# First units of two projections run on rows that the token's norm factor has not touched yet, one core of Trainium2

## The reference, cut to what matters

```python
def rmsnorm(x, w):
    inv = lax.rsqrt(jnp.mean(xf * xf, axis=-1, keepdims=True) + NORM_EPS)
    return (xf * inv) * w

h = rmsnorm(x, norm_mix_w)
a_b, a_c, a_x, z, xbc, dt_raw, g_a, g_b = split_in_proj(h @ w_in)
xbc_c = silu(causal_dwconv(xbc_full, ssd_conv_w) + ssd_conv_b)     # 4 taps
dt = softplus(dt_raw + ssd_dt_bias)                                # 32 heads
...
x = x + merged @ w_o
t = rmsnorm(x, norm_ffn_w)
q = (t @ w_q).reshape(..., PEER_HEADS, 2, PEER_HALF)               # then top 16 of 128 keys, experts
...
y = rmsnorm(x, norm_final_w)
```

## Time and profile before

| what | value |
|---|---|
| median of 3 runs | 2559.65 us (2555.63 to 2560.34) |
| the profiled execution's own time | 2555.39 us |
| its span, first to last instruction | 2553.4 us |
| mean granted TensorE clock | 0.979 |
| PE busy | 2461.1 us (96%) |
| DVE busy | 1640.5 us (64%) |
| ACT busy | 782.9 us (31%) |
| POOL busy | 1437.7 us (56%) |

### The profile page before, as it was taken

How to read it: one execution, slowest core, us unless ns; L and a number is a source line. 1 busy time by engine, 2 the same in 40 slices (tenths; PEclk the granted TensorE clock), 3 DMA queues, 4 the chain that set the end, 5 groups by cost and what they waited for, 6 DMA issues and landing times.

```text
span 2553.4 us, 38043 instructions
## 1 busy us (share of the span) xinstructions
PE 2461.1 (96%) x14490; PEld 2258.2 (88%) x14490; DVE 1640.5 (64%) x2612; ACT 782.9 (31%) x1188; POOL 1437.7 (56%) x787
## 2 busy tenths in 40 slices
PE   7899999999989998999999999999999999999997
PEld 6899899996678997999999999999988999999986
DVE  5787344545487423127988969889587666666663
ACT  2222112321112101123333345565533333332331
POOL 3455333432143454446766767777766777777762
PEclk8899999999999998999999999999999999999998
DMA  3223222224464232225766758988987888888861
GB/s 130 75 83 128 98 92 87 91 91 157 160 222 137 72 113 74 83 91 186 260 243 232 263 200 275 297 299 294 297 323 286 329 312 309 310 324 312 312 242 62
DMA packets 206252, 507.49 MB, mean 199 GB/s; under 512 B 15008, under 2 KB 103456, under 8 KB 203680
## 3 DMA queue, kind: packets, MB, share of 16 engines
q1 hardware_dynamic: 56496, 204.76, 25.0%
q10 hardware_dynamic: 112752, 166.56, 18.3%
q0 software_dynamic: 36864, 134.23, 14.2%
HBM read 422.06 MB, written 83.44 MB: 198 GB/s over the span
## 4 chain that ended last, share of the span: by engine, by line
PE 89%; DVE 6%; issue 2%; DMA 1%; ACT 1%; ACTq 0%; POOL 0%; DVEq 0%; POOLq 0%
PE ps L797 47%; PE ps L565 29%; PE ps L845 4%; PE ps L704 1%; PE ps L734 1%; PE ps L712 1%; PE ps L591 1%; DVE abuf L1732 1%; PE ps L810 1%; PE ps L716 1%; PE ps L719 1%; PE ps L692 0%; DMA gate_scratch<-gt 0%; DVE sp L1344 0%; DMA gbuf<-gate_scratch 0%
## 5 line engine op out<-in xcount | busy, mean ns | idle before, releaser
L514 POOL TENSOR_SCALAR w_hi<-raw 128x1024 fp32r<-128x1024 f32 x129 | 141.3, 1095 | 639.9 <-issue 508.5
L541 POOL TENSOR_TENSOR w_lo<-raw,w_hi 128x1024 fp32r<-128x1024 f32 x128 | 325.8, 2545 | 196.5 <-PE ps L797 196.3
L541 POOL TENSOR_TENSOR w_lo<-raw,e_hi 128x1024 fp32r<-128x1024 f32 x128 | 326.4, 2550 | 186.6 <-PE ps L797 179.7
L797 PE MATMUL ps<-p_hi,w_lo 128*128 128x448 f32 x1024 | 377.1, 368 | 0.0
L797 PE MATMUL ps<-g_hi,w_lo 128*128 128x448 f32 x1024 | 376.5, 368 | 0.0
L516 POOL TENSOR_TENSOR w_lo<-raw,w_hi 128x1024 fp32r<-128x1024 f32 x129 | 320.4, 2483 | 10.8
L565 PE MATMUL ps<-h_hi,w_hi 128*128 128x296 f32 (+1 forms) x1296 | 297.5, 311 | 18.6 <-ACT stage L941 9.6
L565 PE MATMUL ps<-h_lo,w_hi 128*128 128x296 f32 (+1 forms) x1296 | 283.1, 300 | 0.0
L565 PE MATMUL ps<-h_hi,w_lo 128*128 128x296 f32 (+1 forms) x1296 | 282.2, 299 | 0.0
L565 PEld LDWEIGHTS ps<-h_hi,w_hi 128*128 128x128 f32 x1296 | 212.5, 192 | 42.1 <-issue 24.5
L1118 ACT ACTIVATE e_hi<-raw 128x1024 fp32r<-128x1024 f32 x128 | 135.8, 1061 | 299.3 <-PE ps L797 117.1
(11 more groups left out here) (286 smaller groups left out, 5312.9 us busy)
## 6 DMA issues: line engine op xcount, KB each, us to landing
raw<-units SPq DMA_DIRECT2D x385, 512.0 KB, 3.7
gate_scratch<-gt ACTq DMA_DIRECT2D x14, 2048.0 KB, 12.7
gbuf<-gate_scratch ACTq DMA_DIRECT2D x32, 896.0 KB, 8.4
activation_scratch<-ge ACTq DMA_DIRECT2D x120, 224.0 KB, 3.1
abuf<-activation_scratch ACTq DMA_DIRECT2D x30, 896.0 KB, 5.9
prev<-ssm_in ACTq DMA_DIRECT2D x8, 1024.0 KB, 5.7
ssm_s<-prev ACTq DMA_DIRECT2D x8, 1024.0 KB, 4.4
parked_tiles<-stage ACTq DMA_DIRECT2D x24, 296.0 KB, 2.1
```

The lines of the kernel that those rows point to most:

```text
L514: pool.tensor_scalar(w_hi[:, s, :], raw[:, r, :], 1.0, 1.0, ALU.mult, ALU.mult).then_inc(s_whi, 1)
L541: pool.tensor_tensor(w_lo[:, n % 2, :], raw[:, n % RAW, :], e_hi[m % HS_].bitcast(F32), ALU.subtract)\
L797: last = mm(accp[par], w[:, k * P:(k + 1) * P], x_[:, k, t0:t0 + ND], start=k == 0 and i == 0, stop=k == KT - 1 and i == 2)
```

## The change

It touches the first norm, the norm ahead of the queries, and, through shared helpers, the last norm.

1. **Start.** The input loads are put in another order, with unit 0 ahead of x. x also comes token-major (`x_rows`, five tiles of 128 tokens by 1024). ACT makes `hu_hi` = x * w (rounded) and DVE `hu_lo`; no factor is in them. PE issues 20 matmuls of 128 x 128 on ones, then runs units 0 to 4 on `hu`. ACT squares the token-major rows with an accumulator output, which gives each token's sum at once on its own partition. `spread_out(0)` stands in the middle of unit 2. The factor is multiplied into dt (four pieces, L1447) and into the four parked tiles (`scale_stage`) by DVE. `normed` runs beside units 2 to 4, and units from 5 on use h as before.
2. **Softplus** is computed on 128 x 148 tiles (four token quarters on four groups of 32 partitions).
3. **ACT's order** is stage 0, hi parts 0 and 1, bias, abs and exp of dt, then hi parts, stages and stores in turn, and only then the wait for `s_sp`. The first convolution tap moves from DVE to ACT (L1030).
4. **Queries.** `gu_hi` (ACT) and `gu_lo` (DVE) are made while w_o still runs. Units 0 to 3 of w_q run on them; ACT copies them to `qu`, and DVE multiplies them by the factor after `normed`.
5. **Sums** ahead of the queries and at the end: `added_squares` contracts the 128 channels and turns in one step of eight small matmuls; the sum over ones, the row and `turn` are gone there.

```diff
@@ sync
+            sp_.dma_start(col[:], cols).then_inc(s_col, 16)
+            sp_.dma_start(raw[:, 0, :], units[0]).then_inc(ld[0], 16)
             for i in range(4):
                 sp_.dma_start(x[:, 2 * i:2 * i + 2], xT[:, 2 * i:2 * i + 2]).then_inc(s_x[i], 16)
+            sp_.dma_start(raw[:, 1, :], units[1]).then_inc(ld[1], 16)
+            for i in range(XR):
+                sp_.dma_start(rows[i][:], x_rows[:, i]).then_inc(s_xt[i], 16)
...
@@ tensor
             def added_squares(r):
                 pe.wait_ge(s_sqa, KT * (r - GROUPS))
-                for h in range(2):
-                    last = mm(ssp[:, h, 0:HK], ones, sqa[:, h * HK:(h + 1) * HK], start=True, stop=True)
-                last.then_inc(s_ss, 1)
+                nq = TK // NT
+                for i in range(NT):
+                    last = mm(turned[0:nq, i:i + 1], sqa[:, i * nq:(i + 1) * nq], ones[:, 0:1], start=True, stop=True)
+                last.then_inc(s_turn, 1)
...
-            square_sums(0)
-            turn(0)
+            for i in range(WARM):
+                mm(ps[:, 7, 0:P], ones_r[:], ones_r[:], start=True, stop=True)
+            hu = (hu_hi, hu_lo)
+            as_ready(U_DT, U_DT, hu, s_u, 0)
+            tile(U_DT + 1, U_DT + 1, *hu)
+            part(U_DT + 2, 0, 4, hu)
             spread_out(0)
-            two_tiles(U_DT, U_DT, (h_hi, h_lo), 0)
+            part(U_DT + 2, 4, KT, hu)
+            for n in range(U_DT + 3, N_RAW):
+                tile(n, n, *hu)
+            as_ready(N_RAW, N_RAW, (h_hi, h_lo), s_h, 0)
...
@@ scalar
+            def unscaled_hi(w, k, out):
+                act.activation(out[:, k, :], x[:, k, T - out.shape[2]:], ACT.Copy, scale=c_(w, k)).then_inc(s_uhi, 1)
...
+            for i in range(XR):
+                act.wait_ge(s_xt[i], 16)
+                act.activation(rows[i][:], rows[i][:], ACT.Square, accum_out=ss0[:, i:i + 1]).then_inc(s_us, 1)
...
@@ vector
+            def unscaled_lo(i0, w, k, hi, lo):
+                dve.wait_ge(s_uhi, i0 + k + 1)
+                stt(lo[:, k, :], x[:, k, T - lo.shape[2]:], c_(w, k), hi[:, k, :].bitcast(F32), ALU.mult, ALU.subtract)\
+                    .then_inc(s_u, 1)
...
+            def scale_stage(b):
+                n = PARKED[b]
+                dve.wait_ge(s_accf[n % 2], n // 2 + 1)
+                a = halves(stage[b % 2][:])
+                tt_(a, a, inv[:], ALU.mult).then_inc(s_scl, 1)
...
-            link(ts_(sp[1][:], sp[2][:], 2.0, None, ALU.add))
+            link(ts_(pk[1][:], pk[2][:], 2.0, None, ALU.add))
...
@@ vector, w_o and queries
+                if j >= 1:
+                    unscaled_lo(KT, "ffn", j - 1, gu_hi, gu_lo)
+            unscaled_lo(KT, "ffn", KT - 1, gu_hi, gu_lo)
             add_squares(1 + GROUPS, KT - 1)
...
             normed(1, "ffn", g_lo, g_hi)
+            for j in range(Q_RAW):
+                dve.wait_ge(s_qu, j + 1)
+                link(tt_(halves(q[:, j, :]), halves(qu[:, j, :]), inv[:, :, 0:HK], ALU.mult))
```

More of the change, by code:

```diff
@@ L217, in trunk @@
         dq = scr("dq", [P, T])
-        sp = [at(f"sp{i}", R_C + i * TW, [HEADS, T]) for i in range(4)]
         reset = scr("reset", [HEADS, T])
@@ L776, in _ @@
                 tile(U_WO + j, L_WO + j, m_hi, m_lo)
-            added_squares(1 + GROUPS)
-            turn(1 + GROUPS)
-            spread_out(1 + GROUPS)
-            two_tiles(U_WQ, U_WQ - L_SHIFT, (g_hi, g_lo), KT)
-            for j in range(2, N_WQ):
-                tile(U_WQ + j, U_WQ - L_SHIFT + j, g_hi, g_lo)
+            gu, L = (gu_hi, gu_lo), U_WQ - L_SHIFT
+            for k in range(KT):
+                if k == 6:
+                    added_squares(1 + GROUPS)
+                pe.wait_ge(s_u, KT + k + 1)
+                part(U_WQ, k, k + 1, gu, L)
+            part(U_WQ + 1, 0, 4, gu, L + 1)
+            spread_out(1 + GROUPS)
+            part(U_WQ + 1, 4, KT, gu, L + 1)
+            for j in range(2, Q_RAW):
+                tile(U_WQ + j, L + j, *gu)
+            as_ready(U_WQ + Q_RAW, L + Q_RAW, (g_hi, g_lo), s_h, KT)
+            for j in range(Q_RAW + 1, N_WQ):
+                tile(U_WQ + j, L + j, g_hi, g_lo)
             pe.wait_ge(s_q, N_WQ)
@@ new lines, in _ @@
+            dve.wait_ge(s_c, 1)
+            for k in range(KT):
+                unscaled_lo(0, "mix", k, hu_hi, hu_lo)
+            v, i, w = (root0[:, k, :] for k in range(3))
+            dve.wait_ge(s_us, XR)
+            ts_(v, ss0[:], 1.0 / D, EPS, ALU.mult, ALU.add).then_inc(s_vt, 1)
+            inverse_root(0, v, i, w)
+            n = T // P
+            diagonals(P, n, i[:, 0:n])
+            tt_(spread[:, n * P:T], ident[:, 0:T - n * P], i[:, n:n + 1].to_broadcast([P, T - n * P]), ALU.mult)\
+                .then_inc(s_diag, 1)
@@ new lines, in _, with scale_parked @@
+            dve.memset(reset[:], 1.0)
+            dve.wait_ge(s_inv, 1)
+            dve.wait_ge(s_accf[0], 1)
+            wq = T // 4
+            for i in range(4):
+                last = tt_(pk[0][HEADS * i:HEADS * (i + 1), :], sp[0][:, i * wq:(i + 1) * wq],
+                           inv[0:HEADS, i // 2, i % 2 * wq:(i % 2 + 1) * wq], ALU.mult)
+            last.then_inc(s_dts, 1)
+            def scale_parked(k):
+                b = {0: 0, 4: 1, 7: 2}.get(k)
+                if b is None:
+                    return
+                scale_stage(b)
```

274 lines of the change are left out of this document (168 added, 106 removed).

## The result

| | before | changed |
|---|---|---|
| median of the runs, us | 2559.99 (4 runs, 2555.63 to 2562.20) | 2519.93 (4 runs, 2515.88 to 2524.06) |
| profiled execution, us (span) | 2555.39 (2553.4) | 2517.11 (2515.1) |
| PE busy, us (share of the span) | 2461.1 (96%) | 2445.0 (97%) |

The ratio is 0.9846, with a 95% interval of 0.9822 to 0.9869. Measured again later, five runs of the changed kernel had 2518.23 us in the median. Forecast were 2525.6 us and a range of 2511 to 2538.

What follows compares the result with a forecast made beforehand. PE was taken to bound the kernel (89% of the chain that ended last); 13.4 (start) + 17.5 (queries) + 3.1 (end) = 34.0 us, taken from the median 2559.65, gave 2525.6 us, range 2511 to 2538.

Steps and rivals of the forecast that it cites:

- All behind PE, three places.: Whole kernel: only PE's time counts, and the change gains at the start, queries and end, 34.0 us in all.
- Part 1: Start, until the factor is spread at 30.8 us: factor ready by about 27 at most, covered by its place in unit 2.
- Part 2: Start, DVE from the spreading through softplus: chain ends at 71.6 us, PE idles about 13.7, gain 13.4 us.
- The softplus gets 10 us shorter and the chain ends hardly sooner.: Start, DVE: packed softplus 6.8 us instead of 16.3 free of holds, yet the chain ends at 71.6 against 72.39.
- Part 3: Queries: the third query unit starts at 1017.8 us instead of 1035.29, gain 17.5 us.
- No reserve: Queries, fifth unit, first on g: starts at 1030.6 us as `normed` ends near 1031, no wait but nothing spare.
- Part 4: End: the sum over ones and the row go, gain 3.1 us; the new small matmuls take the old 2.09 us.
- At nothing: Costs put at zero: parts made during w_o, first tap on ACT, four query scalings, 20 ones matmuls, 2.6 MB of token rows.
- B: Start: POOL's holds on DVE are mild, chain ends at 60.1 us; 45.7 us gained in all, 2514 us; chance 0.20.
- C: Start: unit 1 and half of unit 2 run at the low clock, factor late; 26.0 us gained, 2533.7 us; chance 0.23.
- D: xBC loop: convolution becomes the bound, gain gone at 1.4 us per unit, 2569 us at 1.8; chance 0.04.
- E: Start and queries: the time only moves, up to 34 us of unseen further waits; chance 0.03.

Runs made afterwards that it cites:

- run 4: The changed kernel with the factor's spreading on PE moved from the middle of unit 2 to ahead of it; 2512.32 us, ratio 0.9804 to the kernel before.
- run 7: The changed kernel with POOL's splits of units 3 to 9 made for only 16 of their 1024 columns; 2509.25 us in one execution.
- run 2: The changed kernel with only the softplus packing undone, its steps on 32x592 again; 2524.98 us, ratio 0.9864 to the kernel before.
- run 10: The changed kernel with the query and last-norm sums of squares made by a row and its turn again; 2524.64 us, ratio 0.9853 to the kernel before.
- run 9: The changed kernel with only the first tap of each convolution back from ACT to DVE; 2519.08 us, ratio 0.9847 to the kernel before.
- run 8: The changed kernel without the twenty matmuls of ones ahead of unit 0; 2523.97 us, ratio 0.9837 to the kernel before.

## Why the prediction was right, step by step

- **"All behind PE, three places."** Right: the three terms give 36.7 of the 38.3 us, and every sign named for it was seen. The sum was 34.0 us, the medians lie 40.1 apart: the terms of the start and of the queries were taken too small (below), and the forecast was 5.7 us above the median.
- **Part 1, loads and factor.** Unit 0 was there at 5.51 us (5.5), unit 1 at 12.75 (12.8), the last token rows at 20.27 (20.4). Unit 0 ended near 19.5, unit 1 at 25.9, the spreading at 30.2 (19.7, 26.3, 30.8). Between 9 and 20 us the queue moved 402 to 418 GB/s, so scaling sizes by the earlier trace's rate was safe, and the 358 GB/s of the Trainium skill (DMA: Bandwidth & Descriptors, "Where 436 GB/s comes from") would have been the worse guide. The factor's matrix was ready at 25.45. The ones ended at 8.11 us, not near 6, still ahead of the first parts. The cover held, and was longer than needed: run 4 took 3.3 us out of it.
- **Part 2, the chain.** Taken 29.3 us of work and 11.5 us of holds from 30.8 on. Measured (run 7 beside the changed kernel): 28.8 and 10.6, from 30.2 on. It ended at 69.6, not 71.6, each piece a little shorter. The stop was 12.19 us against 13.7. The term was 13.4 and is 15.7: right in mechanism, 2.3 us small.
- **"The softplus gets 10 us shorter and the chain ends hardly sooner."** It ended 2.8 us sooner. What packing is worth within the change is 6.35 us (run 2), since the same five splits hold the long chain and the short one.
- **Part 3, queries.** Term 17.5, measured 17.4 to the third unit's start, which came 18.0 us behind w_o against 17.9 in the sum. That closeness is luck. The steps were taken too long: the sums came 6.2 us behind w_o and not 6.6, the small matmuls took 1.25 and 1.20 us in the two profiles and not 2.08. At the high clock the third unit comes 16.4 us behind w_o (second profile); here a low clock behind the pause, which I had let cancel, brought it back to 18.0. Nor could it cancel in this measure: the low clock of before stands behind 1035.29, in the third unit. To that unit's end the queries gained 18.9 us in this profile and 20.4 in the second, so the term was 1.4 to 2.9 us small. "No reserve" at the fifth unit was too dark: its last g part was there at 1014.6, a us before the unit began, and is used as the unit's last eighth; run 10 moved the factor and caused no stop.
- **Part 4, end.** 3.1 taken; 3.6 in one profile (small matmuls 1.55 us) and 3.1 in the other (2.08, as taken).
- **At nothing.** The tap (run 9), the work beside w_o (units 6.40 us apart) and the ones (run 8) cost nothing. The ones also bring nothing that the trace shows, which I had not said.
- **Rivals.** B (holds mild) is refuted by run 7: holds are 10.6 us. C: unit 0 did start at the low pace, but paced by DVE it lost nothing; units 1 and 2 ran fast. D: lines stay 6.55 us apart with the tap on either engine. E: no new wait took the gain.
